# Up projection of the first block with the activations stationary, its result turned in 32x32 blocks through memory ahead of the convolution

## The reference, cut to what matters

```
def conv_gated_mlp(u, w_up, conv_w, conv_b, w_down):
    S = u.shape[1]
    up = u @ w_up
    pad = jnp.pad(up, ((0, 0), (CONV_WIDTH - 1, 0), (0, 0)))
    up = conv_b + sum(pad[:, j:j + S] * conv_w[j] for j in range(CONV_WIDTH))
    gate, val = jnp.split(up, 2, axis=-1)
    return (jax.nn.gelu(gate, approximate=True) * val) @ w_down

y = conv_gated_mlp(rms_norm(h, ln_ffn_pre[l]), w_up[l], conv_w[l], conv_b[l], w_down[l])
h = h + rms_norm(y, ln_ffn_post[l])
```

## Time and profile before

| | |
|---|---|
| median of 3 runs | 2459.01 us (2458.68 to 2463.18) |
| the profiled execution, its own time | 2457.88 us |
| its span, first to last instruction | 2456.2 us |
| granted TensorE clock, mean | 0.999 of full |
| PE busy | 2440.6 us, 99% |
| weight loads on PE | 2086.3 us, 85% |
| VectorE busy | 1413.5 us, 58% |
| ACT busy | 1111.2 us, 45% |
| GpSimd busy | 155.8 us, 6% |
| DMA | 480.98 MB, mean 196 GB/s |

### The profile page before, as it was taken

The page is one execution under the profiler, slowest core; times in us unless marked ns, Lnnn a source line. Parts: engine busy times, 40 slices in busy tenths (PEclk is TensorE's granted clock), DMA queues, the critical chain, the costliest instruction groups (busy, mean ns, idle before and its releaser), DMA issues.

```text
span 2456.2 us, 30361 instructions
## 1 busy us (share of the span) xinstructions
PE 2440.6 (99%) x12508; PEld 2086.3 (85%) x12508; DVE 1413.5 (58%) x1112; ACT 1111.2 (45%) x985; POOL 155.8 (6%) x140
## 2 busy tenths in 40 slices
PE   9999999999999999999999999999999999999998
PEld 8999888888888888888888889888888888888886
DVE  6877645676667766444555574654544445444455
ACT  5534554654454544333454363444343443433344
POOL 4000000011212112000000000000010100000000
PEclk9999999999999999999999999999999999999999
DMA  7545555556455465655565554556666766665544
GB/s 254 185 157 168 171 175 187 176 186 222 171 191 206 155 226 196 243 189 194 217 228 175 190 172 166 176 188 207 224 218 206 227 216 221 229 208 193 193 173 154
DMA packets 239874, 480.98 MB, mean 196 GB/s; under 512 B 8566, under 2 KB 17708, under 8 KB 238892
## 3 DMA queue, kind: packets, MB, share of 16 engines
q1 hardware_dynamic: 239352, 479.42, 57.7%
q10 hardware_dynamic: 436, 0.30, 0.0%
HBM read 467.63 MB, written 12.06 MB: 195 GB/s over the span
## 4 chain that ended last, share of the span: by engine, by line
PE 98%; ACT 1%; DVE 0%; DMA 0%; issue 0%; SPq 0%; DVEq 0%; ACTq 0%
PE ps L1143 21%; PE ps L1145 21%; PE ps L1144 21%; PE ps L1128 17%; PE ps L1129 9%; PE ps L1136 2%; PE ps L1137 2%; PE ps L1135 2%; PE ps L1101 1%; PE ps L1386 1%; ACT w_hi L608 0%; DVE w_lo L1595 0%; DMA raw<-in_w_in_dram 0%; PE ps L1393 0%; PE ps L1534 0%
## 5 line engine op out<-in xcount | busy, mean ns | idle before, releaser
L1595 DVE TENSOR_TENSOR w_lo<-raw,w_hi 128x2048 fp32r<-128x2048 f32 x427 | 978.9, 2292 | 997.4 <-ACT w_hi L608 996.9
L608 ACT ACTIVATE w_hi<-raw 128x2048 fp32r<-128x2048 f32 x427 | 818.7, 1917 | 1291.1 <-PE ps L1145 873.8
L1128 PE MATMUL ps<-xa,w_hi 128*128 128x512 f32 x1664 | 578.5, 392 | 0.4 <-DVE w_lo L1595 0.3
L1143 PE MATMUL ps<-w_hi,g 128*128 128x512 f32 x1216 | 475.1, 391 | 0.0
L1145 PE MATMUL ps<-w_hi,g 128*128 128x512 f32 x1216 | 473.3, 389 | 0.0
L1144 PE MATMUL ps<-w_lo,g 128*128 128x512 f32 x1216 | 473.1, 389 | 0.0
L1129 PE MATMUL ps<-xa,w_lo 128*128 128x256 f32 x1664 | 465.2, 280 | 0.0
L1143 PE MATMUL ps<-w_hi,xa 128*128 128x512 f32 x1024 | 399.5, 390 | 0.3 <-DVE w_lo L1595 0.3
L1145 PE MATMUL ps<-w_hi,xa 128*128 128x512 f32 x1024 | 398.5, 389 | 0.0
L1144 PE MATMUL ps<-w_lo,xa 128*128 128x512 f32 x1024 | 398.4, 389 | 0.0
L1128 PEld LDWEIGHTS ps<-xa,w_hi 128*128 128x128 f32 x1664 | 311.3, 187 | 69.7 <-issue 0.6
(11 more groups left out here) (319 smaller groups left out, 1751.2 us busy)
## 6 DMA issues: line engine op xcount, KB each, us to landing
raw<-in_ffn_w_dram SPq DMA_DIRECT2D x132, 1024.0 KB, 5.1
raw<-in_w_in_dram SPq DMA_DIRECT2D x95, 1024.0 KB, 5.1
raw<-in_w_up_dram SPq DMA_DIRECT2D x88, 1024.0 KB, 5.1
raw<-in_w_down_dram SPq DMA_DIRECT2D x44, 1024.0 KB, 5.1
raw<-in_w_out_dram SPq DMA_DIRECT2D x32, 1024.0 KB, 5.0
raw<-in_w_pg_dram SPq DMA_DIRECT2D x16, 1024.0 KB, 6.4
raw<-in_pl_w_gate_dram SPq DMA_DIRECT2D x16, 1024.0 KB, 5.8
turned_rows<-ff SPq DMA_DIRECT2D x11, 512.0 KB, 3.7
```

What stands on the lines that cost most here:

```text
L608: A(w_hi[j % SPLIT][:, :], raw[s][:, :], ACT.Copy).then_inc(sem("w_hi_ready"), 1)
L1128: mm(ps[:, 4 * gr + n, :], hi[:, k, w], x, start=begin, stop=False)
L1143: mm(o, high, hi, start=begin, stop=False)
L1595: V.tensor_tensor(w_lo[j % SPLIT][:, :], raw[j % RAW][:, :], w_hi[j % SPLIT][:, :].bitcast(F32), ALU.subtract).then_inc(sem("w_lo_ready"), 1)
```

## The change

In up the matmuls take the form of glu (`by_rows`): "up" leaves `COLUMN_PHASES` and `SPREAD`. The tokens' scale becomes a number for each partition (`norm_scale`, shared with glu), and `spread_scale` goes for up. Both halves, gate and value, are turned like glu's product, but ahead of the convolution:
- ACT evacuates two banks with the scale into `up_rows` (`up_evacuation`), at positions 3 and 7.
- VectorE turns the blocks (`turn_up`), where `summed_up` stood.
- SyncE stores them and loads them back as four DMAs: the first half at positions 1 and 2 of the next iteration, the second half at positions 5 and 6.
- ACT spreads them into `ff_sum` (`up_columns`): the first half at position 6 of the same iteration of ACT, the second at position 2 of the next.
- The convolution, the gelu and the product's copy come later, most in the iteration after; the taps have positions of their own on VectorE. GpSimd's product goes to `ff_sum[1]`.

The three buffers for this are three quarters of `h`. So `h` (3 x 512 KB) is stored to memory at SyncE's position 6 of the first iteration (`put_h`), and taken back in down1 (`take_h`). down1's table `at` shifts accordingly. Semaphores are shared between up and glu (`blocks_turned` for `glu_turned`), with UP_TURNS = 22 ahead of glu's counts.

```diff
-COLUMN_PHASES = ("up", "in2")
+UP_TURNS = 22
+COLUMN_PHASES = ("in2",)
...
-SPREAD = {"in1": 1, "up": 2, "in2": 3}
+SPREAD = {"in1": 1, "in2": 2}
...
+        h_parts = [x_in[:, 1024 * n:1024 * (n + 1)] for n in range(3)]
+        up_rows, up_block_turned, up_staged = h_parts[0].rearrange("p (a c) -> p a c", a=2), h_parts[1], h_parts[2]
...
+            def put_up_blocks(i, gr):
+
+                sp.wait_ge(sem("blocks_turned"), i * 2 + (gr + 1))
+                sp.dma_start(up_turned_dram, up_block_turned).then_inc(sem("blocks_stored"), 16)
+
+            def take_up_blocks(i, gr):
+
+                sp.wait_ge(sem("blocks_stored"), i * 32 + (16 * gr + 16))
+                for j in range(4):
+                    sp.dma_start(block_rows(up_staged, j), block_column(up_turned_dram, j)).then_inc(sem("blocks_loaded"), 16)
+
+            def put_h(i):
+
+                if isinstance(i, int) and i == 0:
+                    sp.wait_ge(sem("turned"), TURNED["up"] + 4)
+                    sp.wait_ge(sem("rows_squared"), ROWS_SQUARED["up"] + 4)
+                    for n in range(3):
+                        sp.dma_start(h_dram[n], h_parts[n]).then_inc(sem(f"h_put{min(n, 1)}"), 16)
+                else:
+                    take_up_blocks(i - 1, 1)
...
-            columns("up", [(t["w_up"][0], 0), (t["w_up"][0], FF)], 512, peel=1,
+            columns("up", [(t["w_up"][0], 0), (t["w_up"][0], FF)], 512, peel=2,
+                    at={1: earlier(lambda i: put_up_blocks(i - 1, 0)), 2: earlier(lambda i: take_up_blocks(i - 1, 0)),
+                        5: earlier(lambda i: put_up_blocks(i - 1, 1)), 6: put_h},
                     after=lambda i: put_away("pe1") if isinstance(i, int) and i == 0 else None)
...
+            def up_evacuation(i, gr):
+                act.wait_ge(sem("chunks_multiplied"), done("up", i, 4 * gr + 3))
+                act.wait_ge(sem("up_scale_ready"), 1)
+                if isinstance(i, int) and (i, gr) == (0, 0):
+                    act.wait_ge(sem("h_put0"), 16)
+                else:
+                    act.wait_ge(sem("blocks_turned"), i * 2 + gr)
+                for a in range(2):
+                    last = A(up_rows[:, a, :], bank(2 * gr + a), ACT.Copy, scale=tok[:, NORMS["up"] + 12 + a:NORMS["up"] + 13 + a])
+                last.then_inc(sem("up_rows"), 1)
+
+            def up_columns(i, gr):
+                act.wait_ge(sem("blocks_loaded"), i * 128 + (64 * gr + 64))
+                if not (isinstance(i, int) and i == 0):
+                    act.wait_ge(*((sem("up_low"), i) if gr else (sem("up_conv0"), i * 8)))
+                for a in range(2):
+                    last = A(in_blocks(ff_sum[gr][:, :, a * P:(a + 1) * P]), staged_half(up_staged, a), ACT.Copy)
+                last.then_inc(sem(f"up_summed{gr}"), 1)
...
-            stream("up", {0: lambda i: (first(lambda: token_roots("up"))(i), earlier_affine(i)),
-                          2: earlier_high, 4: affine("up", 0), 5: gelu_gate},
+            stream("up", {0: lambda i: (first(lambda: token_roots("up"))(i), earlier(affine("up", 0))(i)),
+                          2: earlier(second_values), 3: lambda i: (up_evacuation(i, 0), earlier(gelu_gate)(i)),
+                          6: lambda i: up_columns(i, 0), 7: lambda i: (up_evacuation(i, 1), earlier_high(i))},
                    peel=1, started=True)
...
+            def turn_up(i, gr):
+
+                dve.wait_ge(sem("up_rows"), i * 2 + (gr + 1))
...
+                for a in range(2):
+                    last = V.transpose(block_columns(up_block_turned, a), up_rows[:, a, :].rearrange("p (k j c) -> p k j c", k=4, c=32))
+                last.then_inc(sem("blocks_turned"), 1)
...
+            stream("up", turn_up, peel=1, started=True,
+                   at={0: first(lambda: row_sums("up")), 1: lambda i: (first(lambda: norm_scale("up"))(i), earlier_tap(0, 1)(i)),
+                       2: earlier_tap(0, 2), 4: earlier_tap(1, 1), 5: earlier_tap(1, 2)})
```

More of the change, by code:

```diff
@@ L219, in halves_of, with block_columns, staged_half @@
             return ap.rearrange("p (a c) -> p a c", a=2)
[L221 to L227, removed]
+        def block_columns(turned, a):
+            return turned.rearrange("p (j a k r) -> p a k j r", j=4, a=2, r=32)[:, a]
+        def staged_half(blocks, a):
+            return blocks.rearrange("p (i a k r) -> p a k i r", i=4, a=2, r=32)[:, a]
         def in_blocks(ap):
@@ L424, in earlier, with take_h @@
+            def take_h(i):
+                sp.wait_ge(sem("up_summed1"), plan["up"]["iters"])
+                for n in range(3):
+                    sp.dma_start(h_parts[n], h_dram[n]).then_inc(sem("h_back"), 16)
             def earlier(f):
@@ L868, in f @@
                     act.wait_ge(sem(f"{ph}_summed{gr}"), i + 1)
+                    if not (isinstance(i, int) and i == 0):
+                        act.wait_ge(sem("up_product"), i)
                     for n in range(4):
@@ L889, in glu_high @@
             def glu_high(i):
[L890 removed]
+                act.wait_ge(sem("blocks_loaded"), i * 64 + 64 * (UP_TURNS + 1))
                 for a in range(2):
[L892 removed]
+                    last = A(in_blocks(g[:, bass.ds(i * 4, 4), a * P:(a + 1) * P]), staged_half(staged, a), ACT.Copy)
                 last.then_inc(sem("glu_high"), 1)
@@ L1646, in mixed_add @@
                 dve.wait_ge(sem("mixed_read"), 4 * (name == "down1") + q + 1)
+                if name == "down1":
+                    dve.wait_ge(sem("h_back"), 48)
                 for a in range(2):
@@ new lines, in convolve @@
+            def convolve(i, gr, tap):
+                for n in range(4):
+                    if tap == 1:
+                        dve.wait_ge(sem(f"up_tap{gr}"), i * 4 + (n + 1))
+                    else:
+                        dve.wait_ge(sem(f"up_conv{gr}"), i * 8 + (n + 1))
+                    c = i * 4 + (44 * gr + n + col[f"conv_w{2 - tap}"])
+                    V.scalar_tensor_tensor(ff_out[gr][:, n, tap:S], ff_sum[gr][:, n, 0:S - tap], cols[:, bass.ds(c, 1)],
+                                           ff_out[gr][:, n, tap:S], ALU.mult, ALU.add).then_inc(sem(f"up_conv{gr}"), 1)
@@ L2273, in glu_product @@
                 dve.wait_ge(sem("glu_gate_ready"), i + 1)
-                if not (isinstance(i, int) and i == 0):
-                    dve.wait_ge(sem("glu_turned"), i)
+                dve.wait_ge(sem("blocks_turned"), i + UP_TURNS)
                 for a in range(2):
```

119 lines of the change are left out of this document (56 added, 63 removed).

## The result

The changed kernel takes **2495.4 us** (2490.8 to 2498.9, four runs), the kernel before beside it 2459.2: ratio 1.0143, interval 1.0122 to 1.0163, slower by 36 us. I had forecast slower, 2468.4 us, range 2454 to 2478. The sign is right and the size is not.

What follows compares the result with a forecast made beforehand. PE, busy 99% of the span, was taken as the bound, with ACT and VectorE second. 2457.9 - 9.6 (matmuls) + 19 (stalls) = 2467.3; with the median 1.1 higher, 2468.4 us, range 2454 to 2478.

Steps and rivals of the forecast that it cites:

- The matmuls: In up, 24 row matmuls of 512 columns replace 16 pairs per chunk; gain 9.6 us.
- The place and cause of the wait: PE stands at the second chunk of iterations 2 to 11, because the first half's block loads queue behind a held weight load.
- blocks in time: Rival in up: the last block lands 3.7 us after issue, PE does not stand; 2449.4 us, chance 0.12.
- The length of the wait: PE's stall at up's second chunk: 1.9 us each, 0.8 with both lower ends, 2.6 with both upper ones.
- N1's load to the first block load: On SyncE, from loading the next iteration's second chunk to the first block load: 1.2 us, between 0.6 and 1.4.
- last issue to last landing: In up, the last of four block loads lands 5.7 us after issue, between median 5.2 and largest 6.2.
- the embeds' store: 2048 KB write behind a load, 11.5 us; from it, up's 512 KB store lands 6.8 us after the weight load ahead.
- gaps above 3 us: Sign of being wrong: such PE gaps would mean the block loads share the engines with the weights behind them.
- 10 x 1.9 = 19 us: Added wait in up: PE stalls 1.9 us, ten times, in iterations 2 to 11; 19 us in the sum.
- What I had put at 0: Steady-iteration work of VectorE, ACT (two table loads included) and GpSimd, and up's start and end: 0 us added.
- the 0.1 us to spare: After up's stall ACT readies the next low part in 5.3 us against PE's 5.44, so nothing is added.
- ACT too full as well: Rival in up: ACT loses half a microsecond at two places, adding 10 us to the stall; 2478 us, chance 0.08.

Runs made afterwards that it cites:

- experiment 2: Changed kernel with SyncE storing and fetching the first half's blocks one chunk position earlier: 2449.5 us, ratio to the kernel before 0.9965.
- experiment 1: Changed kernel with up's weight loads, from the second iteration on, held four chunks behind VectorE's low parts instead of two: 2449.5 us, ratio 0.9964.
- Experiment 3: Changed kernel with SyncE waiting until the first half's four block loads land before issuing the two weight loads behind them: 2484.2 us, ratio 1.0100.
- experiment 6: Changed kernel with both the wait for landed blocks and the 16 identity transposes on PE: 2476.0 us, ratio 1.0068.
- experiment 4: Changed kernel with 16 unused identity transposes on PE before the second chunk's wait, from up's second iteration on: 2480.4 us, ratio 1.0090.
- e11: Changed kernel with the first half's blocks stored at SyncE's position 0 instead of 1, still fetched at position 2: 2463.1 us, ratio 1.0020.
- Experiment 8: Changed kernel with a distance of three chunks instead of two in up's weight loads: 2452.2 us, ratio 0.9977.
- e10: Changed kernel with the first half's blocks fetched at SyncE's position 1, right behind their store, instead of position 2: 2468.2 us, ratio 1.0048.
- experiments 5 and 9: Changed kernel with up's loop entered with gelu's table, removing 20 table loads: 2493.8 us (5); the same plus a weight-load distance of four: 2449.8 us (9).

## Why the prediction was wrong in size

**The matmuls, right.** Gain 9.6 us forecast. Without gaps up is 9.2 us shorter than before, and the 24 row matmuls of a chunk start 0.227 us apart. By an estimate from the isolated gap that the Trainium skill gives, page "TensorE: Matmul & The Clock Gate", section "Back-to-back issue gap", the gain would have been 2.4 us (2.7 when the sum in the prediction is redone); the traces do not agree, and they decide.

**The place and cause of the wait, right.** The second chunk of iterations 2 to 11, ended by VectorE's low part, through ACT at the first half's blocks, none at the second half's and none at down1. Putting the take ahead of N1's load (experiment 2) or letting that load go (experiment 1) ends it. The case "blocks in time" had 2449.4 us; both measured 2449.5. That they meet to 0.1 us is luck in part: the kernel before ran at 2458.2 beside these runs, not at 2459.0, and against it they gained 8.7 us, not 9.6.

**The length of the wait, too short.** I took 1.9 us (0.8 to 2.6) and it is 2.9, beyond the end that I had called the upper one. Term by term, means of ten iterations:

| term | forecast | measured |
|---|---|---|
| N1's load to the first block load | 1.2 | 1.59 |
| first to last of the four | 1.32 | 1.38 |
| last issue to last landing | 5.7 | 6.34 |
| landing to PE | 5.4 | 5.36 |

The first row lies a little above the end that I had worked out from the embeds' store and then not taken: I set 1.2 between 0.6 and 1.4, and the store landed 7.0 us after N0's load where that estimate said 6.8. The third lies above 6.2, the largest of the 44 block loads of glu that I used as the upper end. In glu the next weight load went 2 to 3 us behind the blocks; here two went right behind, since the hold on N1's load had let them fall due. Experiment 3 prices this at 0.7 us, and its 5.65 is my 5.7; experiment 6 against 4 prices it at 0.4. It is no rule: in experiments 2 and 11, where the store had landed and N1's load went 0.5 us ahead, the blocks take 5.6 us both with no load for 3.3 us behind them and with two right behind. Experiment 8 has 6.3 with one load 1.9 us behind; there, as in the changed kernel, the store was still under way when N1's load went. No run varied these apart. I had named the loads behind as the meaning of gaps above 3 us (four of ten were), and not put them into the range. Ten times 1.0 us is 10 of the 27 us that I was off.

The Trainium skill, page "DMA: Bandwidth & Descriptors", section "Anatomy of one DMA — SWDGE (gpsimd) path", gives a fit by which I had estimated 2.3 us for such a load. The nearest that any run shows is e10's 2.87 us, with the way ahead clear; in the changed kernel it was 6.34, and the measurement decides.

**The clock, missing.** The term "10 x 1.9 = 19 us" let a gap of PE cost its length, and put nothing for what follows it. Nine of ten gaps cost 1.3 to 2.5 us more each, 15 us in all; experiment 4 gave 13 of them back with the wait nearly unchanged. The profile of before could not show it in up, which had no such gap, but the sum had no sentence on it either, and that is the step that failed most: with the restart behind each gap it is 16 of the 27 us. 2449.5 + 29.3 + 15.9 = 2494.7, where 2495.4 was measured.

**What I had put at 0 stayed at 0.** ACT with two table loads an iteration (experiments 5 and 9), VectorE's transposes, GpSimd, and down1's tail: with the blocks in time the measured time is the sum without any of them, to 1 us. Nor is there a second gap behind the first one in any iteration of the changed kernel, as the 0.1 us to spare had said. h is put away between 480.9 and 481.8, landed after 2.6 to 5.0 us, and nobody waited. The rival "ACT too full as well" gave 2478, the figure nearest to the result, by a mechanism that did not happen.

**Not settled.** Whether experiments 3 and 4 add. What makes the blocks land in 6.3 us instead of 5.6, beyond the share of the loads behind. And when a gap brings the clock down in this kernel; its length alone does not tell: after gaps of 1.06 to 2.53 us in experiments 10 and 11 (twenty of them) no matmul ran at the lower level, after gaps of 1.9 and 2.1 us in experiment 3 some did.

## What to carry to other kernels

When a transfer has to be in time, write down everything that stands ahead of it on its queue with its own hold, and what goes right behind it: here two weight loads ahead, with a hold that did not concern the blocks, turned a gain of 9 us into a loss of 36, and moving two entries of a table by one position restored it. Compare the whole issue order with that of the stage from which the form was borrowed, down to the distances; a landing time taken from there holds only with the same neighbours. Price a gap of PE at its length, and give the slow matmuls that may follow it a term or a rival of their own: here 1.3 to 2.5 us behind nine gaps of ten, and nothing behind the gaps of 1.1 to 2.5 us in experiments 8, 10 and 11.

## What the runs showed of the hardware

- Behind PE gaps of 2.3 to 4.5 us in the changed kernel the matmuls start 0.43 us apart, the level of 1.2 GHz, 6 to 12 times, then 0.227 again; 1.3 to 2.5 us for each gap. Those 0.43 us apart begin up to 1.3 us after the gap's end. With transposes of an identity in the gap (e4) nine gaps of 2.0 to 3.3 us keep the level of 2.4 GHz.
- The same four block loads of 128 KB, from the last issue to the last landing: 2.87 us where the weight load ahead had landed before the first was issued (e10), though weight loads follow 0.7 us behind; 4.7 with 1 MB issued 2.4 us ahead (e1); 5.6 with 1 MB issued 0.5 us ahead, whether no load follows for 3.3 us (e2) or two follow within 1.2 (e11); 6.3 with N1's load 1.6 us ahead, issued while the store was under way, and two loads right behind (the changed kernel; two of ten took 7.5), 5.65 without those two (e3).
- The store of 512 KB lands in 3.0 us (median) where no weight load was issued in the 5 us ahead of it (the changed kernel's second halves, e1), in 5.5 where three went together 5 us ahead (e3's second halves), and in 6.5 where it goes 0.5 us behind one.
